# A GpSimd wait for VectorE's last latent split, ahead of the column sums of the later modulation vectors

## The chip, the cores and the metric

The kernel runs on one core of a Trainium2 chip. The metric is the device time of one execution in microseconds (us); lower is better. The core's engines each run their own instruction stream and meet at semaphores: TensorE (PE in the profile; PEld is its weight load), VectorE (DVE), ScalarE (ACT), GpSimd (POOL), and SyncE (SP), which only issues transfers here.

## The reference

Two layers of a diffusion backbone over 1024 latent tokens and 256 context tokens, model width 1024. Each layer has an adaLN modulation: six vectors (shift, scale, gate for the mixer and for the FFN) from one vector-matrix product.

```
m_lat = split(silu(c) @ w_mod[i] + b_mod[i], 6)          # i = 0, 1: 12 vectors of 1024
h_lat = rmsnorm(x_lat) * g_pre_mix * (1 + m_lat[1]) + m_lat[0]
y     = mla_mixer(h_lat, h_ctx, ...)   (layer 0)   |   conformer_conv(h_lat, ...)   (layer 1)
x_lat = x_lat + m_lat[2] * rmsnorm(y)
h     = modulate(rmsnorm(x_lat), m_lat[3], m_lat[4])
x_lat = x_lat + m_lat[5] * rmsnorm(conv_ffn(h, ...))
```

The latent attention of layer 0 projects `h` down (`w_dqkv`: 384 query latents, 128 key/value latents, 64 rotary), normalises these latents and projects them up for each of 8 heads; then softmax attention with 128-query blocks. Everything is fp32.

## The kernel before

Activations lie transposed, model blocks of 128 in the partitions, tokens in the free dimension. Matrix products are made of three fp32r matmuls (high*high, high*low, low*high): ScalarE rounds a tile to its high part, VectorE subtracts for the low part ("split"). `w_hi`/`w_lo`, `h_hi`/`h_lo` and `lat_hi`/`lat_lo` count these parts. `lat_lo` counts the low parts of the latents: two for the key/value side (L1461), then three for the query latents (L1470), five in all.

The twelve modulation vectors (shift, scale, ... of both layers) are computed in two ways. The first two, which the first norm needs, come at once: the scale on TensorE (L2028, counted by `mod_used`), the shift by VectorE's multiply-adds (L1402, L1405) and TensorE's column sums (L1983). The ten later ones, t = 0 to 9, are GpSimd's: for each of 8 row blocks of w_mod it loads 512 KB by a transfer of its own queue (L661 for the first two blocks, L679 for the others), multiplies it by a column of silu(c) in its partitions (L669, L671) and adds it to an accumulator (L672). When `mod_acc` reaches t + 1, TensorE sums the accumulator over the partitions (`mod_sums`, L1983, counted by `mod_mm`) and VectorE adds the bias. There are three accumulators' worth of order: t = 0 waits for `mod_mm` 1, t = 1 for 1, t = 2 for 2, t = 3 for 4, and so on.

TensorE asks for the first of them (`mod_acc` 1) in attention step 2, and for the next two (`mod_acc` 3) in step 4. There are 16 attention steps (8 heads, two halves of the queries); each has four blocks of scores (L2114, L2115 and the three lines of `three`), for which VectorE takes the row maxima (`maxes`, L1503), ScalarE the exponentials (L901), VectorE the scaling of the probabilities (`scales`, L1510 and L1511), TensorE the transposes (L2125), ScalarE and VectorE the split of the transposed (L778, L1517), TensorE the product with the values. Steps 0 and 1 have no product with values. The rotary fold (L2101) comes twice in each step with a new head's queries.

Ahead of attention VectorE makes `h`: for each of 8 blocks of the latents (`h_blocks`, 1024 tokens) the normalised block `ht` (L1379), of which ScalarE makes the high part (L813) and VectorE the low part (L1375); the order on VectorE is ht(k+1), low(k). TensorE's `first_two` follows these blocks: 6 matmuls of weight unit 0 for blocks 0 and 1, and 12 (units 0 and 1) for each later one, then the 12 that are left over. Then VectorE splits weight unit 2 (L1337) and does the same 8 blocks for the context (256 tokens). TensorE waits for all of these, multiplies the context (48 matmuls of 256 columns) and goes on with units 2 to 5, the statistics of the latents (L1957, L1976) and the first head's pieces.

GpSimd's stream begins so (L655 to L661); the diff touches it here:

```python
pool.wait_ge(silu_c, 2)
pool.wait_ge(mod_used, CB)
for t in range(10):
    for k in range(2):
        pool.dma_start(f(F_MD + k * L), modw[t + 2, k]).then_inc(mod_in[k], 16)
```

After the ten sums GpSimd adds squares for the norms and tile sums for the FFN; nothing of it starts before attention is over. The rest of the kernel (output projection, two FFNs, the convolution) is on TensorE's heels in the same manner.

Of the kernel before, what the change touches and what calls it, by code (L numbers as in the profile page):

```python
# [42 lines left out]
QLORA_B = 3  # L43
# [216 lines left out]
def build(nc, xT, ctxT, units, modw, vecs, ident_d, fold_d, cs_d, cosd_d, sind_d, outT):  # L260
# [7 lines left out]
    with ExitStack() as ctx:  # L268
# [13 lines left out]
        def sem(name):  # L282
            return ctx.enter_context(nc.semaphore(name))
# [18 lines left out]
        latent_in, mmx_done, rope_k, lat_scaled, lat_hi, lat_lo = (  # L302
            sem("latent_in"), sem("mmx_done"), sem("rope_k"), sem("lat_scaled"), sem("lat_hi"), sem("lat_lo"))
# [17 lines left out]
        def region(at, n):  # L321

            return next(start for _, start, end in REGIONS if start <= at and at + n <= end)
# [165 lines left out]
        def _(sp):  # L489
# [47 lines left out]
            def load_down(layer, turn, j, gated):  # L537

                d = dn_item(turn, j) + int(gated)
                if d < 8:  # L540
                    sp.wait_ge(w_lo, W_FFN[layer] + 6 + 7 * (MAIN - 2 + d // 4) + 6 + d // 2 % 2)
                else:
                    before = d - 8
                    at = 0 if before < 44 else 1 if before < 66 else 2 if before < 110 else 3
                    was = before - dn_item(at, 0)
                    if at % 2 or was % 2 == 0:
                        i = FB * at + (was if at % 2 else was // 2)
                        sp.wait_ge(w_lo, W_FFN[layer] + 139 + i + 1)
                    else:
                        sp.wait_ge(g_lo, 2 * FB * layer + FB * (at // 2) + was // 2 + 1)  # L550
                s, _, at = dn_landing(layer, d)
                if gated:
                    half = turn // 2
                    sp.wait_ge(g_out, 16 * (FB * layer + j + 1))
                    src = g_d[j][:, half * HALF:(half + 1) * HALF]
                else:
                    src = units[U_FFN[layer] + 2 * FB + j][:, turn % 2 * HALF:(turn % 2 + 1) * HALF]
                sp.dma_start(f(F_RAW + at, HALF), src).then_inc(dn_in[s], 16)
# [91 lines left out]
        def _(pool):  # L650
# [3 lines left out]

            pool.wait_ge(silu_c, 2)  # L655
            pool.wait_ge(mod_used, CB)


            for t in range(10):
# [1283 lines left out]
        def _(pe):  # L1943
# [359 lines left out]
            def ffn(layer, b):  # L2303
# [14 lines left out]
                for p in range(MAIN):  # L2318
                    m, bk = m0 + p, BANKS[p % 2]
                    for i, (_, _, which) in enumerate(PRODUCTS):  # L2320
                        pe.wait_ge(w_lo, w0 + 6 + 7 * p + i + 1)
                        if p == 0:
                            if i in (0, 1, 2):
                                pe.wait_ge(tap_g if i == 0 else tap_v, j0 + 2)
                            if i in (1, 2, 3, 6):
                                pe.wait_ge(b_lo, 16 * layer + {1: 8, 2: 4, 3: 12, 6: 16}[i])
                        elif p == 1 and i < 3:
                            pe.wait_ge(tap_g if i == 0 else tap_v, j0 + 3)
                        elif i == 0:
                            pe.wait_ge(s1_out, 5 * (m - 1))  # L2330
                        elif i == 1:
                            pe.wait_ge(c_new, 2 * (m - 1))
                        elif i == 2:
                            pe.wait_ge(c_new, 2 * (m - 1) - 1)
                        if i in (3, 4, 5, 6):
                            pe.wait_ge(s1_out, 5 * m + {3: 2, 4: 1, 5: 3, 6: 4}[i])
                        start = i < 3
                        for k in range(4):
                            mm = three(bank(bk[which]), half_unit(op_slot(p, i))[k], operands[i][k], start and k == 0, k == 3, True)
                        group_done(mm)  # L2340
# [192 lines left out]
```

## Time and profile before

| | |
|---|---|
| median of 3 runs | 2709.15 us (2703.23 to 2711.56) |
| the profiled execution's own time | 2706.82 us |
| its span in the trace | 2705.0 us |
| TensorE busy | 2574.6 us, 95% |
| VectorE busy | 1948.2 us, 72% |
| GpSimd busy | 902.1 us, 33% |
| share of the last chain on TensorE | 76% |

Busy times are sums over an engine's instructions. The chain is the work that ended last, followed back from the end: at each instruction to what released it or to the one before it on its engine. A TensorE row's duration overlaps the next row's, so its pace is read from the distance between starts.

### The profile page before, as it was taken

What the parts mean: (1) busy time and instruction counts of PE and PEld (TensorE: products, weight loads), DVE (VectorE), ACT (ScalarE), POOL (GpSimd) and SP (SyncE); (2) the same over time, 40 slices, a digit from 0 to 9 for tenths busy, and PEclk for the clock granted to TensorE, in tenths of its full rate; (3) what the DMA queues carried; (4) which work ended last, traced back from release to release, by engine and by line L of the source; (5) the groups of instructions that cost most, each with busy time, mean ns of one, the idle gap of its engine ahead of it and who ended that gap; (6) DMA issues with size and microseconds to landing.
All of it is one profiled execution on the core that took longest, in us unless ns stands there. A gap on an engine that the chain in (4) does not pass through costs nothing.

```text
span 2705.0 us, 31548 instructions
## 1 busy us (share of the span) xinstructions
PE 2574.6 (95%) x11674; PEld 2089.2 (77%) x11674; DVE 1948.2 (72%) x2071; ACT 1141.0 (42%) x1776; POOL 902.1 (33%) x590
## 2 busy tenths in 40 slices
PE   6789999999899999999999989997899999999997
PEld 5667888888687788888888866655787888888886
DVE  5826686867636999999436379997269999995352
ACT  2223444444533555555434232223435555554341
POOL 0801485862021566564001100000134675640001
PEclk9889999999999999999999999996999999999999
DMA  6400232331332222222645310001031222227362
GB/s 256 156 32 22 84 126 93 124 101 39 113 118 77 71 85 87 86 78 102 215 135 173 112 43 32 32 31 62 7 119 55 86 78 86 82 83 225 108 210 81
DMA packets 102356, 263.97 MB, mean 98 GB/s; under 512 B 11088, under 2 KB 12368, under 8 KB 102224
## 3 DMA queue, kind: packets, MB, share of 16 engines
q1 hardware_dynamic: 84496, 201.85, 22.1%
q0 software_dynamic: 11520, 41.95, 4.9%
q10 hardware_dynamic: 6208, 18.42, 1.8%
q8 instruction: 82, 1.34, 0.2%
q14 instruction: 50, 0.41, 0.0%
HBM read 218.13 MB, written 44.04 MB: 97 GB/s over the span
## 4 chain that ended last, share of the span: by engine, by line
PE 76%; DVE 17%; issue 4%; ACT 2%; DMA 1%; POOL 1%; POOLq 0%; ACTq 0%; DVEq 0%; SPq 0%
PE psum L1949 23%; PE psum L1951 22%; PE psum L1950 22%; DVE low L1874 7%; PE psum L2125 2%; PE psum L2200 1%; PE psum L2114 1%; PE psum L2115 1%; PE psum L1983 1%; DVE weights_f32r L1588 1%; DVE acts_f32r L1375 1%; PE psum L2398 1%; DMA low<-ctx_t 1%; DVE small L1503 1%; PE psum L2208 1%
## 5 line engine op out<-in xcount | busy, mean ns | idle before, releaser
L1949 PE MATMUL psum<-acts_f32r,weights_f32r 128*128 128x512 f32 x1760 | 702.5, 399 | 27.0 <-DVE acts_f32r L1375 10.2
L1951 PE MATMUL psum<-acts_f32r,weights_f32r 128*128 128x512 f32 x1760 | 693.1, 394 | 0.0
L1950 PE MATMUL psum<-acts_f32r,weights_f32r 128*128 128x512 f32 x1760 | 692.9, 394 | 0.0
L695 POOL TENSOR_TENSOR low<-low 128x512 f32<-128x512 f32 x70 | 101.5, 1451 | 1117.2 <-ACT low L992 1113.6
L778 ACT ACTIVATE weights_f32r<-low 128x512 fp32r<-128x512 f32 (+1 forms) x498 | 328.7, 669 | 339.9 <-PE psum L1951 261.0
L1949 PEld LDWEIGHTS psum<-acts_f32r,weights_f32r 128*128 128x128 f32 x1760 | 335.8, 191 | 105.0 <-DVE acts_f32r L1375 13.4
L1951 PEld LDWEIGHTS psum<-acts_f32r,weights_f32r 128*128 128x128 f32 x1760 | 334.8, 190 | 71.4
L1950 PEld LDWEIGHTS psum<-acts_f32r,weights_f32r 128*128 128x128 f32 x1760 | 335.5, 191 | 70.0 <-issue 1.9
L1721 DVE TENSOR_TENSOR weights_f32r<-low,weights_f32r 128x512 fp32r<-128x512 f32 x264 | 380.0, 1484 | 0.1
L1728 DVE TENSOR_TENSOR weights_f32r<-low,weights_f32r 128x512 fp32r<-128x512 f32 x176 | 124.5, 712 | 238.2 <-ACT weights_f32r L778 235.2
L722 POOL TENSOR_TENSOR low<-low 128x512 f32<-128x512 f32 x150 | 265.5, 1770 | 39.8 <-DVE acts_f32r L1706 29.3
L1874 DVE SCALAR_TENSOR_TENSOR low<-acts,vectors,low 128x1024 f32<-128x1024 f32 x169 | 203.4, 1277 | 11.6 <-ACT low L778 11.6
L778 ACT ACTIVATE low<-psum 128x512 f32<-128x512 f32 (+1 forms) x242 | 145.6, 601 | 145.3 <-PE psum L1951 144.9
L1949 PE MATMUL psum<-high_f32r,weights_f32r 128*128 128x512 f32 (+1 forms) x472 | 187.2, 397 | 15.7 <-DVE high_f32r L1375 6.9
L1950 PE MATMUL psum<-high_f32r,weights_f32r 128*128 128x512 f32 (+1 forms) x472 | 183.1, 388 | 0.0
L1951 PE MATMUL psum<-high_f32r,weights_f32r 128*128 128x512 f32 (+1 forms) x472 | 183.0, 388 | 0.0
L778 ACT ACTIVATE weights_f32r<-psum 128x512 fp32r<-128x512 f32 x160 | 92.7, 595 | 209.9 <-PE psum L2125 209.9
L1949 PE MATMUL psum<-acts_f32r,high_f32r 128*128 128x512 f32 x320 | 130.9, 409 | 15.7 <-ACT low L901 7.3
L745 POOL TENSOR_TENSOR low<-low 128x512 f32<-128x512 f32 x38 | 60.7, 1597 | 249.8 <-ACT low L778 249.8
L1503 DVE TENSOR_REDUCE small<-psum 128x1 f32<-128x1280 f32 x64 | 95.3, 1489 | 59.1 <-PE psum L2115 58.7
L1081 ACT ACTIVATE low<-low,vectors 128x1024 f32<-128x1024 f32 x76 | 94.6, 1247 | 76.6 <-DVE low L1792 56.1
L1517 DVE TENSOR_TENSOR weights_f32r<-psum,weights_f32r 128x512 fp32r<-128x512 f32 x160 | 107.6, 685 | 22.0 <-ACT weights_f32r L778 21.7
(196 smaller groups left out, 4717.3 us busy)
## 6 DMA issues: line engine op xcount, KB each, us to landing
low<-units SPq DMA_DIRECT2D x134, 512.0 KB, 4.1
low<-units SPq DMA_DIRECT2D x176, 256.0 KB, 3.7
set<-mod_w POOLq DMA_DIRECT2D x80, 512.0 KB, 3.9
gated<-low SPq DMA_DIRECT2D x44, 512.0 KB, 2.6
low<-gated SPq DMA_DIRECT2D x88, 256.0 KB, 4.2
residual<-low SPq DMA_DIRECT2D x48, 256.0 KB, 2.0
acts<-mod_w ACTq DMA_DIRECT2D x8, 1024.0 KB, 16.1
low<-x_t SPq DMA_DIRECT2D x4, 1024.0 KB, 27.8
```

The costliest lines, as they stand in the source:

```text
L695: pool.tensor_tensor(acc, first, ring(n), ADD).then_inc(sq_added, 1)
L722: pool.tensor_tensor(f(to[part - 1], HALF), x, y, op).then_inc(s_new, 1)
L778: return act.activation(out, in_, ACT.Copy, scale=scale)
L1081: act.activation(f(at), src, ACT.Identity, scale=V[:, wv + 2 * FB + c:wv + 2 * FB + c + 1], bias=V[:, wb + c:wb + c + 1]).then_inc(tap_mid, 1)
L1503: chain(dve.reduce_max(S[:, C_MX + c:C_MX + c + 1], PS[:, 0:KEYS], AX.X))
L1517: dve.tensor_tensor(r(at + HALF, HALF), bank(3 + kbn % 2), r(at, HALF), SUB).then_inc(tp_lo, 1)
L1721: dve.tensor_tensor(r(at + HALF, HALF), src, r(at, HALF), SUB).then_inc(w_lo, 1)
L1728: dve.tensor_tensor(r(at + HALF, HALF), dn_raw(layer, dn_item(turn, j)), r(at, HALF), SUB).then_inc(w_lo, 1)
L1874: chain.lag(dve.scalar_tensor_tensor(out=chained, in0=U[i % 2][:, t:t + L], scalar=V[:, V_WDW + t * CB + i:V_WDW + t * CB + i + 1], in1=ch ...
L1949: pe.matmul(out, wl, xh, start=first, stop=False, skip_group_check=continued)
L1950: pe.matmul(out, wh, xl, start=False, stop=False, skip_group_check=continued)
L1951: return pe.matmul(out, wh, xh, start=False, stop=last, skip_group_check=continued)
```

## The change

One line: before its first transfer, GpSimd also waits until VectorE has made the fifth and last low part of the latents (`lat_lo` = QLORA_B + 2 = 5).

```diff
             pool.wait_ge(silu_c, 2)
             pool.wait_ge(mod_used, CB)
+            pool.wait_ge(lat_lo, QLORA_B + 2)
 
 
             for t in range(10):
```

No instruction is added or removed besides the wait. All of GpSimd's work, its 80 transfers included, keeps its order behind it.

## Rows read from the trace of the kernel before

**Rows 1.** The page, busy time: us, share of the span, instructions.

```profile
PE 2574.6 (95%) x11674; PEld 2089.2 (77%) x11674; DVE 1948.2 (72%) x2071; ACT 1141.0 (42%) x1776; POOL 902.1 (33%) x590
```

**Rows 2.** The chain that ended last, 64 to 101 us: start, us, what.

```profile
67.92 1.28 DVE low L1379
69.20 3.23 DVE acts_f32r L1375
72.45 1.28 DVE low L1379
...
97.44 3.10 DVE weights_f32r L1337
```

**Rows 3.** Timeline of GpSimd: start, us, line, operation, tiles, idle before and its releaser.

```profile
68.96 2.37 POOL L672 TENSOR_TENSOR set<-set 128x1024 f32<-128x1024 f32 x1
...
99.76 1.13 POOL L661 DMA_DIRECT2D set<-mod_w  x2 [0.30 <-POOL set L672]
...
137.54 2.40 POOL L672 TENSOR_TENSOR high<-high,set 128x1024 f32<-128x1024 f32 x1
...
261.91 1.12 POOL L669 TENSOR_SCALAR set<-set,small 128x1024 f32<-128x1024 f32 x1 [120.55 <-PE psum L1983]
```

**Rows 4.** Timeline of VectorE, with the same columns.

```profile
49.86 2.47 DVE L1405 SCALAR_TENSOR_TENSOR high<-acts,small,high 128x1024 f32<-128x1024 f32 x2
...
102.03 0.48 DVE L1379 SCALAR_TENSOR_TENSOR low<-low,small,psum 128x256 f32<-128x256 f32 x1
...
102.94 0.48 DVE L1379 SCALAR_TENSOR_TENSOR low<-low,small,psum 128x256 f32<-128x256 f32 x1
...
108.05 2.45 DVE L1375 SCALAR_TENSOR_TENSOR high_f32r<-low,small,high_f32r 128x256 fp32r<-128x256 f32 x2
...
183.44 3.49 DVE L1470 TENSOR_TENSOR acts_f32r<-low,acts_f32r 128x1024 fp32r<-128x1024 f32 x3
```

**Rows 5.** Timeline of TensorE, with the same columns.

```profile
67.94 0.79 PE L1949 MATMUL psum<-acts_f32r,weights_f32r 128*128 128x512 f32 x1 [2.44 <-DVE acts_f32r L1375]
...
110.56 0.58 PE L1949 MATMUL psum<-high_f32r,weights_f32r 128*128 128x256 f32 x1 [6.89 <-DVE high_f32r L1375]
...
114.56 0.29 PE L1949 MATMUL psum<-high_f32r,weights_f32r 128*128 128x256 f32 x1
...
118.16 0.40 PE L1949 MATMUL psum<-acts_f32r,weights_f32r 128*128 128x512 f32 x1
...
129.07 2.29 PE L1957 MATMUL psum<-ones,low 128*128 128x1 f32 x20
```

**Rows 6.** Windows: busy us of PE, PEld, DVE, ACT, POOL; granted clock; DMA; GB/s.

```profile
70.00:80.00 10.00, 6.80 (x16) 4.42 (x15) 9.93 (x5) 2.68 (x3) 9.15 (x7) 0.50 0.35 117
```

**Rows 7.** VectorE's groups by form, 198 to 262 us: busy, mean ns; idle before.

```profile
L1503 DVE TENSOR_REDUCE small<-psum 128x1 f32<-128x1280 f32 x9 | 13.4, 1491 | 15.5 <-PE psum L2115 15.4
L1511 DVE TENSOR_SCALAR low<-low,small 128x1280 f32<-128x1280 f32 x8 | 7.1, 887 | 0.3
...
L1498 DVE TENSOR_TENSOR weights_f32r<-low,weights_f32r 128x1024 fp32r<-128x1024 f32 x1 | 1.2, 1225 | 0.2 <-ACT weights_f32r L778 0.2
```

**Rows 8.** VectorE's groups by form, 461 to 533 us.

```profile
L1511 DVE TENSOR_SCALAR low<-low,small 128x1280 f32<-128x1280 f32 x9 | 15.5, 1725 | 0.3
...
L1498 DVE TENSOR_TENSOR weights_f32r<-low,weights_f32r 128x1024 fp32r<-128x1024 f32 x1 | 3.0, 2983 | 0.0
```

**Rows 9.** The chain that ended last: rotary folds of four later attention steps.

```profile
476.54 0.86 PE psum L2101 x2
509.32 0.86 PE psum L2101 x2
...
609.11 0.86 PE psum L2101 x2
641.47 0.86 PE psum L2101 x2
```

**Rows 10.** The chain that ended last: TensorE's column sums of t = 1 and 2.

```profile
323.47 4.01 PE psum L1983 x32
```

## The prediction

> **What bounds the kernel now.** I read the page first, then the chain that ended last from 45 to 265 us, then the timelines of VectorE, GpSimd and TensorE over the same stretch. TensorE is busy 95% of the span [rows 1], so the time to gain is where TensorE stands still. The chain shows such a place: from 64 to 110 us it runs almost wholly on VectorE [rows 2]. TensorE gets the first block of `h` at 67.94, then works in bursts, and before the context matmuls at 110.56 it is idle for 6.89 us, released by VectorE's last low part [rows 5].
>
> In this stretch VectorE is slow. Between two `ht` (L1379) lie 72.45 - 67.92 = 4.53 us; `ht` itself takes 1.28, and the low part (L1375) 3.23 [rows 2]. The same operation on the same shape (scalar_tensor_tensor, two inputs in SBUF, 128x1024) took 2.47 us for two, about 1.24 each, at 50 us, when GpSimd had not begun [rows 4]. The difference fits GpSimd's rhythm. Its addition at 68.96 ends at 71.33 [rows 3]; the low part that starts at 69.20 ends at 72.43, that is 1.1 us after GpSimd's end: it waited out the addition and then ran. Seven such blocks have the same picture.
>
> After 110.56 the chain is on TensorE (context, units 2 to 5) until about 170 us, then a short tail over all engines, and VectorE's last low part of the latents ends at 183.44 + 3.49 = 186.9 [rows 4]. GpSimd meanwhile has finished t = 0 and t = 1 at 137.54 + 2.40 = 139.9 and stands for 120.55 us until TensorE has taken t = 0 in step 2 [rows 3]. So the two sums that slow VectorE down are made some 100 us before anybody wants them.
>
> **What the change does, part by part.**
>
> *It removes GpSimd from 48 to 187 us.* First VectorE's latent blocks. Undisturbed, `ht` and a low part take 2.47 [rows 4] plus some 0.03 of waiting on its own semaphore: 2.50 a pair. The third `ht` starts at 67.92 as before. Six pairs bring the low part of block 6 to 67.92 + 15.0 = 82.9; the last low part has to wait for ScalarE's high part (1.15 us a block in ScalarE's timeline, within the pair's 2.50) and ends at about 84.1. Then come the shift's bias and the split of unit 2, which ran from 97.44 for 3.10 us [rows 2] and took 1.23 undisturbed, by the like operation L1498 [rows 7]: it ends at about 85.6, against 100.54 before. The context blocks took from there to 108.05 + 2.45 = 110.50, 10.0 us [rows 4]. Their undisturbed pitch stands in the trace: 102.94 - 102.03 = 0.91 [rows 4]. First high part and `ht` 1.0, then seven low parts at 0.91 and the last, 7.5 in all: 93.1.
>
> TensorE has to keep up. `first_two` is 96 matmuls of 512 columns. At the full clock 48 of them took 129.07 - 118.16 = 10.91, 0.227 each [rows 5]. At the half clock 18 matmuls of 256 columns started in the 4.00 us from 110.56 to 114.56 [rows 5], 0.43 for 512. Now TensorE has the half clock all through 70 to 80 us (granted 0.50) [rows 6], since it stops after each block. With a block every 2.50 us, 6 matmuls at half clock take 2.6 and it does not stop. I take that the clock rises after 4 us of unbroken work, as it did from 110.56: then block 1 is done at 72.5, each later block costs 12 x 0.227 = 2.73, and the end is 72.9 + 6 x 2.73 + 2.73 = 92.0. That is 1.1 us before the context blocks, so VectorE still sets the moment, 93.2. Saved there: 110.56 - 93.2 = 17.4 us. Of the idle time only some 1.1 us is left, less than the pauses of 1.5 us at 84 to 95 us, through which the granted clock stayed at 0.98 to 1.00 in the windows. So the context matmuls should run at the full clock: 48 x 0.119 = 5.7 us instead of 118.16 - 110.56 = 7.6 [rows 5], 1.9 more. Sum: **19.3 us** earlier at unit 2. If the clock is low again it is 17.4.
>
> From 118 to 187 us nothing changes but the date. VectorE's operations that GpSimd disturbed there (120 to 137 us) are hidden behind TensorE, which had no gap. The things that could become late now: unit 3 and 4's transfers (issued when a slot is free, 4.3 us to land, needed 25 and more us later), the rotary tables (issued by ScalarE right after it copies the first result, 4.5 us to land, at about 99, needed at 110). None binds. GpSimd's own 16 transfers leave this stretch, which can only help.
>
> *It moves GpSimd's work to 168 us.* The last low part is now at 186.9 - 19.3 = 167.6. Behind the waiting instruction stand all transfers and sums; who waits for them is TensorE's column sums. One sum, t = 1, took from its first transfer at 99.76 to 139.94, 40.2 us with a disturbing VectorE [rows 3]. So t = 0 is ready at 208, t = 1 at 248, t = 2 at 288. They are wanted: t = 0 shortly before 261.91, when TensorE had summed it [rows 3], some 1.7 us of sums earlier, and 17 us less, at about 243; t = 1 and 2 at 323.47 [rows 10], less 17, at 306. Slack 35 and 18 us. t = 2 also waits for `mod_mm` 2, at 245, before 248. From t = 3 on GpSimd again waits for TensorE and all is as before. In time nothing is late.
>
> *The price: steps 0 and 1 of attention are now disturbed.* GpSimd was idle there, and now runs from 168 to 288 without a break. VectorE's operations with a PSUM input are no slower beside GpSimd (L1503, 1.49; L1517, 0.68 in either kind of stretch). Two operations are: `scales` (L1511), 0.887 undisturbed and 1.725 disturbed, and the split of a head's weights (L1498), 1.23 and 2.98 [rows 7, 8]. Steps 0 and 1 have eight and one: 8 x 0.84 + 1.75 = 8.5 us of VectorE's time. How much of it is on the path? In steps of full length hardly any: from fold to fold the step at 476.54, with GpSimd working, took 32.78, and the step at 609.11, with GpSimd idle for half of it, 32.36 [rows 9]. Steps 0 and 1 lack work on TensorE and are a chain of scores, maxima, exponentials; but VectorE waits for the scores 8 times, 15.4 us together, 5.7 of it the first time [rows 7], so about 1.4 per block is left as cover, with none in front of one of them (the one behind L1498). I take 1.5 us for that block, and 0.2 for each of the seven others, for the times when an operation waits longer than its cover: 3 us. The bounds are 0 and 8.5, and in the worst case each L1511 waits out a whole addition of 2.4.
>
> The skill has a rule on this that speaks against the change. The Trainium skill, "SBUF — State Buffer", section "Who interferes with whom", says that VectorE and GpSimd share one port pair with an exclusive lock: the later instruction blocks completely until the earlier one is done, and this holds for VectorE's two-input operations from SBUF and for its fast modes. The trace agrees: 3.23 us for the low part that met an addition, 1.24 without. By the lock at its worst all eight `scales` would meet one; the measured mean says that they meet about a third of it.
>
> *Sum.* 19.3 - 3.0 = 16.3 us. The profiled execution's own time was 2706.82: 2690.5. The median of the three runs is 2.3 above that execution, in a spread of 8.3; I say **2691**.
>
> **The rivals.**
>
> A. *Only part of the gain* (0.12). TensorE takes over as the bound in `first_two`: its clock does not rise at once, or falls again. Were it at half clock all through, 96 x 0.43 = 41 us from 67.94 would end at 109, and nearly nothing is left of the gain; with a rise at 80 as now, 28 matmuls are done by then and 68 more take 15.4, end 95.5, 2.4 late, and the context runs cold: about 15 - 3 = 12, 2695 to 2697. For it: the half clock of [rows 6]. Against: that clock goes with the pauses which the change takes away, and it rose 4.0 us after 110.56 [rows 5].
>
> B. *The disturbance is moved, not removed* (slower or even; 0.07). In steps 0 and 1 an L1511 that starts just behind an addition waits for all of it, 2.4 us; VectorE is in order, so the next maximum is late, so the exponential, so the scores. 8 x 2.4 + 1.75 = 21 us, less nothing if TensorE has no other work, makes 2706.8 - 19.3 + 21 = 2708.5. It decides the sign from 2.2 us a block on. Against: a mean of 0.84 in 9 disturbed cases [rows 8] and about 1.4 of cover.
>
> C. *The sums come too late* (slower; 0.03). If a sum takes over 46 us instead of 40.2, TensorE waits at 306 for t = 2; with 52 us a sum it waits 18 us, the whole gain, and beyond that the kernel is slower. For it: GpSimd now meets VectorE in every step. Against: t = 2 to 9 were made in attention, and take 37 us in GpSimd's timeline.
>
> D. *No effect* (0.03): VectorE is slow here for another reason than GpSimd. Then about 2707. Against: the durations beside GpSimd's, one by one.
>
> **How the numbers follow.** My forecast has 0.75: 2686 to 2696, from the price of 0 to 8.5 and the clock's 1.9, and the spread of runs. Rival A 0.12 (2695 to 2702), B 0.07 (2700 to 2712), C 0.03, D 0.03. The range that holds 8 in 10 is 2684 to 2700. A measurement of this kernel tells 0.3%, 8.1 us, from no change. Faster by that: the forecast and most of A, 0.84. Within: part of A and B, D, 0.11. Slower: the worse part of B and C, 0.05.
>
> **What the profile after would show.** L1375 at 1.3 us a block from 67 us on, and L1337 at 1.2; the context matmuls starting at 93 us and unit 2 at 99; TensorE's granted clock over 0.9 from 72 us on; GpSimd's first L669 at about 171 us; L1511 in steps 0 and 1 at a mean of 1.7; the column sums at 243 and 307 with no wait for GpSimd. I am wrong if TensorE's last matmul of `first_two` comes after 94 us (A), if steps 0 and 1 take more than 8 us longer (B), or if a column sum waits (C).

## The result and the profile after

The changed kernel took 2688.84 us in the median of 7 runs (2684.0 to 2694.01), the kernel before 2709.15 (2703.23 to 2711.79, 7 runs). The ratio is 0.9924, interval [0.9908, 0.9941]: 0.8% faster, 20.3 us by the medians. Forecast were 2691 and a range of 2684 to 2700. The profiled execution has a span of 2687.0 us against 2705.0: 18.0 us less.

The line of the page that answers to [rows 1]; VectorE's busy time is 13.9 us lower with the same instructions:

```profile
PE 2567.0 (96%) x11674; PEld 2085.8 (78%) x11674; DVE 1934.3 (72%) x2071; ACT 1140.9 (42%) x1776; POOL 897.9 (33%) x590
```

All line numbers are one higher from here on. VectorE's timeline in the `h` blocks, the answer to [rows 2] and [rows 4]:

```profile
68.01 1.28 DVE L1380 SCALAR_TENSOR_TENSOR low<-low,small,psum 128x1024 f32<-128x1024 f32 x1
69.21 1.28 DVE L1376 SCALAR_TENSOR_TENSOR acts_f32r<-low,small,acts_f32r 128x1024 fp32r<-128x1024 f32 x1
70.53 1.28 DVE L1380 SCALAR_TENSOR_TENSOR low<-low,small,psum 128x1024 f32<-128x1024 f32 x1
...
81.78 2.59 DVE L1376 SCALAR_TENSOR_TENSOR acts_f32r<-low,small,acts_f32r 128x1024 fp32r<-128x1024 f32 x2
...
84.60 1.23 DVE L1338 TENSOR_TENSOR weights_f32r<-low,weights_f32r 128x1024 fp32r<-128x1024 f32 x1
```

The low part takes 1.28 us instead of 3.23, the pair 70.53 - 68.01 = 2.52, the split of unit 2 1.23 instead of 3.10. TensorE's timeline, the answer to [rows 5], and below it the windows that answer to [rows 6]:

```profile
68.03 0.80 PE L1950 MATMUL psum<-acts_f32r,weights_f32r 128*128 128x512 f32 x1 [2.10 <-DVE acts_f32r L1376]
...
92.00 0.39 PE L1952 MATMUL psum<-acts_f32r,weights_f32r 128*128 128x512 f32 x1
93.48 0.39 PE L1950 MATMUL psum<-high_f32r,weights_f32r 128*128 128x256 f32 x1 [1.09 <-DVE high_f32r L1376]
...
99.33 0.40 PE L1950 MATMUL psum<-acts_f32r,weights_f32r 128*128 128x512 f32 x1
...
110.24 2.29 PE L1958 MATMUL psum<-ones,low 128*128 128x1 f32 x20
```

```profile
70.00:80.00 10.00, 9.44 (x40) 7.29 (x39) 9.86 (x9) 4.56 (x5) 0.00 (x0) 0.94 0.01 2
80.00:90.00 10.00, 10.00 (x46) 8.29 (x45) 9.58 (x15) 4.91 (x8) 0.00 (x0) 1.00 0.18 52
90.00:100.00 10.00, 8.91 (x62) 8.08 (x61) 6.02 (x12) 5.36 (x9) 0.00 (x0) 1.00 0.47 160
```

TensorE's wait ahead of the context has shrunk from 6.89 to 1.09 us, and the granted clock from 70 to 80 us is 0.94 instead of 0.50. GpSimd's timeline, the answer to [rows 3]:

```profile
166.66 1.29 POOL L662 DMA_DIRECT2D set<-mod_w  x2 [166.20 <-DVE acts_f32r L1471]
...
204.00 1.13 POOL L662 DMA_DIRECT2D set<-mod_w  x2 [0.30 <-POOL set L673]
...
241.46 1.74 POOL L662 DMA_DIRECT2D set<-mod_w  x2 [0.30 <-POOL high L673]
...
279.11 1.13 POOL L662 DMA_DIRECT2D set<-mod_w  x2 [0.30 <-POOL set L673]
...
305.61 1.12 POOL L670 TENSOR_SCALAR set<-set,small 128x1024 f32<-128x1024 f32 x1 [25.38 <-PE psum L1984]
```

It starts when VectorE's last low part is done and works until 279, with pauses of at most 2.9 us for its own transfers. Then it waits for TensorE, not TensorE for it. VectorE's groups by form from 176 to 242 us, the stretch that was undisturbed in [rows 7]:

```profile
L1504 DVE TENSOR_REDUCE small<-psum 128x1 f32<-128x1280 f32 x9 | 13.4, 1488 | 11.0 <-PE psum L2116 11.0
L1512 DVE TENSOR_SCALAR low<-low,small 128x1280 f32<-128x1280 f32 x8 | 12.3, 1542 | 0.3
...
L1499 DVE TENSOR_TENSOR weights_f32r<-low,weights_f32r 128x1024 fp32r<-128x1024 f32 x1 | 2.4, 2432 | 0.2 <-ACT weights_f32r L779 0.2
```

The scaling of the probabilities has gone from 0.887 to 1.54 us and the split of the head's weights from 1.23 to 2.43: the disturbance is here now.

**Where the 18.0 us lie.** The instructions and their order are the same in both traces, so each VectorE and ScalarE instruction can be set against itself. The table gives by how many us it starts earlier than in the first trace of before, as the median over the stretch (times of the kernel before; of an even number of instructions, the upper of the two in the middle). Three traces are of the changed kernel itself, one is a second of the kernel before; the others are told of below.

| stretch, us | before, 2nd | changed | changed, 2nd | changed, 3rd | wait_h | t1_late |
|---|---|---|---|---|---|---|
| 98 to 103 | 0.1 | 14.7 | 14.7 | 14.6 | 14.6 | 14.6 |
| 110 to 120 | -0.1 | 18.8 | 18.9 | 18.7 | 18.7 | 18.7 |
| 150 to 165 | -0.1 | 20.4 | 20.4 | 20.3 | 20.3 | 18.7 |
| 200 to 215 (step 0) | 0.1 | 22.0 | 20.3 | 20.1 | 19.1 | 20.2 |
| 240 to 270 (step 2) | 0.1 | 22.4 | 15.8 | 15.7 | 19.1 | 20.3 |
| 600 to 700 | 3.2 | 22.9 | 21.6 | 19.7 | 18.7 | 26.7 |
| 1870 to 1895 | -0.1 | 23.1 | 20.0 | 19.8 | 15.1 | 25.1 |
| 1930 to 2000 | 0.1 | 19.7 | 20.0 | 16.4 | 15.6 | 23.9 |
| 2600 to 2650 | 0.0 | 19.7 | 20.0 | 16.4 | 12.1 | 20.4 |

The gain is complete before attention and is the same in all three traces of the changed kernel, 20.3 to 20.4 us. One run more bears on it: `late_start` of experiment 3 does the same work as the changed kernel up to 166 us, and it is 19.0 us ahead at 110 to 120 us but 18.9 at 150 to 165. What comes after attention begins moves by several us from one execution to the next, in the kernel before too.

### The profile page after: what moved, and what is told of

It reads as the page before. It is cut to its first block, busy times and chain, and to the rows that moved or that the text cites. A ratio compares the mean times of both kernels' runs of the same rounds, so it can differ in the third digit from the quotient of the medians.

```text
span 2687.0 us, 31548 instructions
## 1 busy us (share of the span) xinstructions
PE 2567.0 (96%) x11674; PEld 2085.8 (78%) x11674; DVE 1934.3 (72%) x2071; ACT 1140.9 (42%) x1776; POOL 897.9 (33%) x590
## 4 chain that ended last, share of the span: by engine, by line
PE 76%; DVE 16%; issue 4%; ACT 2%; DMA 1%; POOL 1%; ACTq 0%; POOLq 0%; DVEq 0%; SPq 0%
PE psum L1950 23%; PE psum L1952 22%; PE psum L1951 22%; DVE low L1875 7%; PE psum L2126 2%; PE psum L2201 1%; PE psum L2115 1%; PE psum L2116 1%; DVE weights_f32r L1589 1%; PE psum L1984 1%; PE psum L2399 1%; DVE small L1504 1%; DMA low<-ctx_t 1%; PE psum L2209 1%; DVE high_f32r L1710 1%
## 5 line engine op out<-in xcount | busy, mean ns | idle before, releaser
L1950 PE MATMUL psum<-acts_f32r,weights_f32r 128*128 128x512 f32 x1760 | 703.2, 400 | 19.3 <-DVE acts_f32r L1648 6.4
L673 POOL TENSOR_TENSOR set<-set 128x1024 f32<-128x1024 f32 x49 | 120.2, 2453 | 4.1
```

Of the source, the lines that this page charges most:

```text
L673: add = pool.tensor_tensor(acc, acc, part, ADD)
L1950: pe.matmul(out, wl, xh, start=first, stop=False, skip_group_check=continued)
```

## The experiments

**1. Which part of GpSimd's work slows VectorE.** Three kernels put a piece of work ahead of the new wait, from 65 us on, and leave the sums after it. Their results are not used. The waits on `mod_in` further down count the transfers that each adds.

Transfers alone:

```diff
+            pool.wait_ge(mod_mm, 1)
+            for k in range(16):
+                if k > 1:
+                    pool.wait_ge(mod_in[k % 2], 16 * (k // 2))
+                pool.dma_start(f(F_MD + (k % 2) * L), modw[2, k % CB]).then_inc(mod_in[k % 2], 16)
+            for k in range(2):
+                pool.wait_ge(mod_in[k], 16 * 8)
             pool.wait_ge(lat_lo, QLORA_B + 2)
```

> The changed kernel, with 16 extra transfers of 512 KB on GpSimd's queue from 65 us on, ahead of the new wait, and no arithmetic; the sums are made later, as in the changed kernel. Theory 1 (GpSimd's arithmetic holds up VectorE's two-input operations): the low parts of h stay at 1.28 us each, the context matmuls start at 93 to 94 us, the time is that of the changed kernel within 2 us (2685 to 2692). Rival (the transfers or the making of their descriptors slow VectorE): the low parts come to 2 us or more and the context matmuls start after 98.

Additions alone, and one-input multiplications alone. Each diff is cut to the work that is added; ahead of it stand two transfers that fill its inputs, the waits for them, and the wait for `mod_mm` 1:

```diff
+            for k in range(12):
+                chain(pool.tensor_tensor(f(F_MD + 2 * L), f(F_MD), f(F_MD + L), ADD))
             pool.wait_ge(lat_lo, QLORA_B + 2)
```

```diff
+            for k in range(24):
+                chain(pool.tensor_scalar(f(F_MD + 2 * L), f(F_MD), S[:, C_SC:C_SC + 1], 1.0, MUL, MUL))
             pool.wait_ge(lat_lo, QLORA_B + 2)
```

> The changed kernel, with 12 extra additions (128x1024, two inputs in SBUF, results not used) on GpSimd from 65 us on, ahead of the new wait, and two transfers before them. Theory 1: each low part beside them waits for the addition that runs, so it takes 2.5 to 3.5 us instead of 1.28; 12 additions of 2.4 us cover 65 to 95 us, and the context matmuls start at 103 to 110 us. Most of the gain of the change is gone: 2695 to 2705. Rival (it was the transfers): the low parts stay at 1.3 and the context starts at 93 to 94.

> The changed kernel, with 24 extra one-input multiplications by a column (128x1024, results not used) on GpSimd from 65 us on, ahead of the new wait, and two transfers before them. Theory 1 in the form that any GpSimd instruction which reads SBUF holds up a two-input operation of VectorE: each low part waits for the rest of one of 1.1 us, 0.6 on average, and takes about 1.9 us; eight of them put the context at 97 to 100 us, 4 to 6 us later than in the changed kernel. Rival: only GpSimd's two-input additions hold VectorE up; then the low parts stay at 1.3 and the context starts at 93 to 94.

The latent low parts (L1383 here) among VectorE's groups by form, 64 to 115 us, and the first context matmul in TensorE's timeline. Transfers:

```profile
L1383 DVE SCALAR_TENSOR_TENSOR acts_f32r<-low,small,acts_f32r 128x1024 fp32r<-128x1024 f32 x8 | 10.2, 1281 | 0.1
```

```profile
93.51 0.38 PE L1957 MATMUL psum<-high_f32r,weights_f32r 128*128 128x256 f32 x1 [1.00 <-DVE high_f32r L1383]
```

Additions, with GpSimd's own row last:

```profile
L1383 DVE SCALAR_TENSOR_TENSOR acts_f32r<-low,small,acts_f32r 128x1024 fp32r<-128x1024 f32 x8 | 17.3, 2167 | 0.0
```

```profile
108.38 0.58 PE L1957 MATMUL psum<-high_f32r,weights_f32r 128*128 128x256 f32 x1 [10.99 <-DVE high_f32r L1383]
```

```profile
67.70 36.93 POOL L663 TENSOR_TENSOR set<-set 128x1024 f32<-128x1024 f32 x12 [17.98 <-PE psum L1991]
```

Multiplications:

```profile
L1383 DVE SCALAR_TENSOR_TENSOR acts_f32r<-low,small,acts_f32r 128x1024 fp32r<-128x1024 f32 x8 | 15.8, 1984 | 0.0
```

```profile
102.36 0.58 PE L1957 MATMUL psum<-high_f32r,weights_f32r 128*128 128x256 f32 x1 [5.95 <-DVE high_f32r L1383]
```

```profile
66.06 37.24 POOL L663 TENSOR_SCALAR set<-set,small 128x1024 f32<-128x1024 f32 x24 [16.31 <-PE psum L1991]
```

Sixteen transfers leave the low part at 1.281 us and the start where the changed kernel has it. The additions put the start back to 108.4, within 2.2 us of the kernel before, and the multiplications to 102.4. So it is the arithmetic, and both kinds of it; the rivals fall. VectorE's `ht`, the same operation on the same shape but with one input in PSUM, stays at 1.28 beside the additions:

```profile
L1387 DVE SCALAR_TENSOR_TENSOR low<-low,small,psum 128x1024 f32<-128x1024 f32 x8 | 10.2, 1280 | 3.7 <-PE psum L1984 3.5
```

My sizes were off in part: the mean beside additions is 2.17, below the 2.5 to 3.5 expected, but the blocking goes both ways, so 12 additions spread over 36.9 us (a mean of 3.01 us for one, not 2.4) and disturbed VectorE longer, into the context blocks. The same holds for the multiplications, 1.46 on average, not 1.12, and their start at 102.4 is later than the 97 to 100 expected.

The times of the three were 2698.19, 2712.74 and 2695.32 us, one execution each. The first and the second are 6 and 8 us above what was expected, and the third is faster than the first although its context starts 9 us later. Part of this is what happened later: in step 1 of attention alone the first two lost 1.8 and 4.1 us and the third gained 0.7 against the kernel before (experiment 4). In the measure of the table the first is 20.4 us ahead at 150 to 165 us, like the changed kernel, and 9.9 at the end; what its other losses come from stays open. The times are therefore no evidence for the theory; the durations and the starts are.

**2. The context blocks by themselves.** GpSimd begins when the latent `h` is done:

```diff
-            pool.wait_ge(lat_lo, QLORA_B + 2)
+            pool.wait_ge(h_lo, CB)
```

> The new wait is put earlier still: GpSimd waits for the low parts of the latent h alone (h_lo 8, at 84 us), so its first products and additions, from about 88 us on, stand beside the eight context blocks only. Port theory: the latent part of the gain stays (VectorE's latent blocks end at 84.4), of the context part (8 blocks, 10.0 us disturbed, 7.5 undisturbed) some 1.5 to 2.5 us are lost, and the context matmuls start at 94.5 to 96 instead of 93.5. Rival (it is the first minutes of GpSimd's work in general, transfers included, that cost): the start falls back to 100 or later.

TensorE's timeline:

```profile
95.95 0.39 PE L1950 MATMUL psum<-high_f32r,weights_f32r 128*128 128x256 f32 x1 [3.50 <-DVE high_f32r L1376]
```

2.5 us later than in the changed kernel, as large as the context's term in the sum (10.0 - 7.5). The time was 2696.42 us, one execution. In the measure of the table it is 14.8 us ahead at 150 to 165 us, 5.6 less than the changed kernel, and not 2.5 less: after the pause of 3.50 us the granted clock was at half speed from 97.1 to 100.5, in the context, and after the column sums again from 117.6 to 121.0. In this execution the longer wait ahead of the context cost more than itself.

**3. How much slack the sums have.** GpSimd begins about 42 us later than in the changed kernel, when it has the fourth exponential of step 0:

```diff
-            pool.wait_ge(lat_lo, QLORA_B + 2)
+            pool.wait_ge(s_free, 4)
```

> The new wait is put later: GpSimd waits for the fourth exponential of attention step 0 (s_free 4, at about 205 us), some 38 us later than in the changed kernel. Rival C of my prediction made real: sum t = 0 would be ready at about 243, wanted at 237.5, so TensorE waits 5 us for it; the sums t = 1 and 2 at about 318 against 303, another 10 to 15 us. Expected 15 to 20 us slower than the changed kernel's 2687 span, 2700 to 2708. If the slack was larger than I read from the rows, TensorE waits less and the time stays under 2695.

The time was 2708.84 us, one execution, the span 2707.0. TensorE's waits from 190 to 400 us (us in total, times, longest), its column sums after the two waits, and GpSimd's transfers for the first three sums:

```profile
PE psum L1984 <- POOL set L673: 13.0, 2, 8.4
```

```profile
245.90 2.30 PE L1984 MATMUL psum<-ones,set 128*128 128x1 f32 x11 [4.58 <-POOL set L673]
...
321.12 3.58 PE L1984 MATMUL psum<-ones,high 128*128 128x1 f32 x16 [8.39 <-POOL set L673]
```

```profile
208.29 1.28 POOL L662 DMA_DIRECT2D set<-mod_w  x2 [207.84 <-ACT low L902]
...
246.14 1.13 POOL L662 DMA_DIRECT2D set<-mod_w  x2 [0.30 <-POOL set L673]
...
284.56 1.13 POOL L662 DMA_DIRECT2D set<-mod_w  x2 [0.30 <-POOL high L673]
```

Rival C is real once the wait is late enough: TensorE waits 4.6 us for t = 0, which was ready at 245.8 and wanted at 241.3 (the column sums of the changed kernel start at 237.5, but step 2 begins 3.7 us later here), and 8.4 us for t = 2, ready at 321.1. In the measure of the table it is 18.7 us ahead of before at 240 to 270 us, 10.7 at 270 to 300, and 0.2 at 340 to 400: the second step is more than the wait, since the clock was at half speed after each wait, from 246.2 to 253.0 and from 317.8 to 331.5 us (the step with the two sums took 46.6 us, against 36.3 in before). In the changed kernel t = 0 was ready at 204 and t = 2 at 279, and TensorE's sums, which stood at 323.47 in [rows 10], began at 301.8; so the slack was 34 and 23 us, near the 35 and 18 of the prediction.

**4. Other places for the two sums, and the price in attention.** Three variants keep the `h` blocks free, and move what meets attention:

```diff
-            pool.wait_ge(lat_lo, QLORA_B + 2)
+            pool.wait_ge(h_lo, 2 * CB)
```

is wait_h; split_sums and t1_late have this and one more wait ahead of the transfers of t = 1:

```diff
             for t in range(10):
+                if t == 1:
+                    pool.wait_ge(lat_lo, QLORA_B + 2)      # split_sums
+                    pool.wait_ge(s_free, 6)                # t1_late, in place of it
                 for k in range(2):
```

> The new wait is put earlier: GpSimd waits for the low parts of h and of the context's h (h_lo 16) instead of the last low part of the latents, so it works from 93 to about 168 us and is idle in attention steps 0 and 1, as before the change. Theory 1 with the price of my prediction: the context matmuls start at 93 to 94 as in the changed kernel; steps 0 and 1 get back what the disturbance cost there (3 us by the prediction, under 1 by the trace after); but t = 1 now meets the tail before attention (152 to 166 us), where VectorE's two-input splits of the latents are on the path, 1 to 4 us. Sum 2684 to 2692, even with the changed kernel within 3 us, and clearly faster than before (ratio about 0.993). Rival (the place of the work in attention is what matters, not the h blocks): it falls back to about 2705.

> t = 0 starts after the low parts of h and of the context's h (h_lo 16, 93 us) and runs beside TensorE-bound work until 131 us; t = 1 waits for the last low part of the latents and runs from 166 to 204 us, beside step 0 only. Port theory: the context starts at 93 to 94 as in the changed kernel, the tail before attention is undisturbed, step 1 of attention is undisturbed. Even with the changed kernel or 1 to 2 us better: 2684 to 2690. The clock's half-speed stretches in attention and later can move it by 5 us either way, as they do between runs of one kernel.

> t = 0 starts after the low parts of h and of the context's h (93 us) and ends at 131; t = 1 waits for the sixth exponential of attention (s_free 6, in the middle of step 1, about 217 us) and ends at about 255, t = 2 at about 292, wanted at 303. So the h blocks, the tail before attention, step 0 and half of step 1 are all undisturbed, and no sum is late. Theory: step 1 takes the 30.1 us that it takes undisturbed, the milestones are 20.4 us ahead of before at 165 us and stay within 1 us of that in steps 1 to 4. Against the changed kernel no difference beyond the spread of runs: 2684 to 2692. Rival (the disturbance of steps 0 and 1 costs several us on average): 2 to 3 us below the changed kernel in the medians of one chip.

The changed kernel and the kernel before were run again:

> The changed kernel itself, once more, with a second trace. Theory 2 (the differences of some us after attention's start, such as the 3.3 us that the changed kernel loses at 1880 us, are where the granted clock happens to fall, not the change): the two traces agree within 0.3 us up to the first stretch at the half clock that only one of them has, and differ by about half of each such stretch from there on, 1.7 or 3.4 us at a time; the spans differ by up to 10 us. Rival (the loss at 1880 us comes from the change): it stands in this trace at the same place.

> The changed kernel itself, timed beside the others on the same chip: median 2684 to 2692, ratio to before 0.991 to 0.994, and a third trace. Up to 165 us it is 20.4 us ahead of before, as in both earlier traces, within 0.3 us. Attention step 1 takes 29.5 to 34.6 us, according to how long its clock is low.

> The kernel before, with a second trace, to see how far its own milestones move. The same theory as for the changed kernel: the disturbed low parts at 2.9 us on average, context matmuls at 110.4 to 110.7; step 1, undisturbed, 30.1 us; differences of 1.7 or 3.4 us where a stretch at the half clock is longer or missing; span 2698 to 2712.

| kernel | median, us (lowest to highest, runs) | ratio to before on its chip |
|---|---|---|
| wait_h | 2693.50 (2685.20 to 2695.49, 6) | 0.9929 [0.9913, 0.9946] |
| split_sums | 2691.78 (2686.84 to 2696.42, 6) | 0.9938 [0.9921, 0.9954] |
| t1_late | 2689.81 (2682.33 to 2692.86, 6) | 0.9934 [0.9915, 0.9952] |
| changed, timed again beside t1_late | 2692.54 (2691.59 to 2698.33, 6) | 0.9951 [0.9933, 0.9968] |
| changed, 2nd trace | 2686.83, one execution | |
| before, 2nd trace | 2706.84, one execution | |

All keep the gain, so the place of the work in attention is not what the change is about. None is shown to be better than the others: the intervals overlap. The changed kernel beside t1_late came out slightly above what was expected (2684 to 2692, ratio 0.991 to 0.994).

What the disturbance costs in attention is read from step 1, from its rotary fold to that of step 2 (L2101 of the kernel before). The windows, with [rows 6]'s columns, of before, then of the changed kernel's first and second trace, then of t1_late, where GpSimd comes in only at the end:

```profile
212.78:242.88 30.10, 26.56 (x139) 22.10 (x140) 18.64 (x29) 11.55 (x20) 0.00 (x0) 0.94 0.06 18
```

```profile
190.80:220.48 29.68, 24.98 (x139) 20.98 (x140) 21.93 (x28) 11.56 (x20) 24.50 (x19) 1.00 0.39 127
```

```profile
192.51:227.10 34.59, 28.90 (x139) 23.92 (x140) 23.02 (x28) 11.56 (x20) 29.01 (x22) 0.85 0.40 126
```

```profile
192.60:222.60 30.00, 26.46 (x140) 22.07 (x141) 18.67 (x29) 11.54 (x20) 1.21 (x2) 0.94 0.06 18
```

Undisturbed, step 1 takes 30.0 to 30.1 us in both traces of before, in wait_h, wait_h8 and t1_late, at a granted clock of 0.94. Disturbed, it takes 29.7 us where the clock stays at full speed and 34.6 where it falls to a mean of 0.85; the third trace of the changed kernel has 34.5, add_early 34.2, xfers_early 31.9, scale_early 29.4. The mean of the changed kernel's three is 32.9, so the price is 2.8 us, and anything from -0.4 to +4.5 in one execution.

Two runs lie in between. In late_start GpSimd's arithmetic begins at 212.3, in the second half of the step, which takes 30.1 us. In split_sums it ends at 204.8 and rests until 245.9; step 1 was expected to be undisturbed there, but its first 12 us are not, and it takes 34.3 us:

```profile
192.59:226.91 34.32, 29.14 (x140) 24.20 (x140) 20.94 (x29) 11.54 (x20) 12.67 (x9) 0.85 0.23 76
```

So GpSimd's work in the rest of the step adds next to nothing (34.3 against 34.6 and 34.5), and the length of the step goes with its granted clock. Whether the disturbance of the first 12 us makes the clock fall, or it would have fallen without it, these runs do not show; the price of 2.8 us is a mean of three executions, and not shown to be due to VectorE's longer operations.

The other places cost too: in wait_h t = 1 meets the tail before attention, and 20.3 us ahead have become 19.1 by step 0. t1_late, which avoids both, keeps its lead through the first steps (later it moves, to 26.7 us and back to 20.4, and not within the 1 us that was expected for steps 1 to 4); it is 2.7 us below the changed kernel by the medians of one chip, in the direction of the price, but not clear of noise.

**5. The loss at 1900 us.** In the first trace of the changed kernel 3.3 us of the lead go between 1895 and 1940 us (of before). There TensorE sums over partitions with 24 one-column matmuls (L2399). Its timeline in the first trace and in the second:

```profile
1878.06 3.14 PE L2399 MATMUL psum<-ones,low 128*128 128x1 f32 x24
1881.06 0.78 PE L1950 MATMUL psum<-acts_f32r,weights_f32r 128*128 128x512 f32 x1
1881.63 0.63 PE L1951 MATMUL psum<-acts_f32r,weights_f32r 128*128 128x512 f32 x1
1882.06 0.63 PE L1952 MATMUL psum<-acts_f32r,weights_f32r 128*128 128x512 f32 x1
```

```profile
1881.04 2.73 PE L2399 MATMUL psum<-ones,low 128*128 128x1 f32 x24
1883.64 0.49 PE L1950 MATMUL psum<-acts_f32r,weights_f32r 128*128 128x512 f32 x1
1883.96 0.40 PE L1951 MATMUL psum<-acts_f32r,weights_f32r 128*128 128x512 f32 x1
1884.20 0.40 PE L1952 MATMUL psum<-acts_f32r,weights_f32r 128*128 128x512 f32 x1
```

After the same instructions the clock is at half speed in one execution (0.43 us from one matmul to the next) and at full speed in the other (0.23). The second trace loses nothing there; the third does. So the loss is no fixed cost of the change: theory 2 stands, the rival of after_again falls. That the change does not make it likelier is not shown: two of its three traces have the loss, and neither of the two of before.

## Why the prediction was right, point by point

**The place and the mechanism** were right. VectorE set the start of the context, and its low parts waited for GpSimd's arithmetic. The rows after and experiment 1 show it: GpSimd's transfers alone do not have the effect, its additions and multiplications do.

**The terms ahead of attention** fit closely. Low part of the last latent block done at 84.4 (84.1 in the sum), split of unit 2 at 85.8 (85.6), last matmul of `first_two` starting at 92.0 (its end put at 92.0), context at 93.5 (93.2), unit 2 at 99.3. 118.16 - 99.33 = 18.8 us against 19.3. Rival A did not come: the clock rose when the pauses were gone, at 71.1 us in the first trace, 3.1 us after the first matmul. The 4 us of the prediction are no constant: in the second trace of the changed kernel the clock rose at 74.0, 6.0 us after the first matmul, and the last of `first_two` started at 92.5. The context still started at 93.45, since VectorE set that moment.

**One thing was missing from this sum.** From 118 to 187 us I had nothing but a shift. The changed kernel is 20.4 us ahead at 150 us, 1.6 more than at 118. After the column sums of the key statistics (L1957 at 129.07 [rows 5]) the clock was at half speed in both traces of before (131.6 to 135.1 us in the first), and in none of the three of the changed kernel. wait_h and t1_late are one and the same up to there, and from 112 to 116 us the granted clock is 1.00 in wait_h and 0.74 in t1_late, which is the one with 18.7 us. late_start, which is the changed kernel up to 166 us, has the half clock from 113.0 to 116.4 and 18.9 us. So the 1.6 us can come and go as the loss of experiment 5 does, and without them the change is worth 18.7 to 19.0 us ahead of attention, within 0.6 of the 19.3 of the sum. Whether the change makes the full clock likelier there stays open.

**The price in attention**, 3 us between 0 and 8.5, was the uncertain term. In the profiled execution it was nothing: the lead grew from 20.4 to 21.9 us by the fold of step 0 and to 22.4 by step 2. Over three traces of the changed kernel step 1 has a mean price of 2.8 us. That this is near 3 is luck: I had put the 3 together from VectorE's cover in front of the maxima, while the single executions have -0.4, 4.5 and 4.4, according to TensorE's clock in the step. Rival B, in which the price grows to the whole gain, did not come; 4.5 us was the most seen in the changed kernel. Rival D, that GpSimd is not what slows VectorE, falls with the durations.

**The deadlines** held, with 34 and 23 us to spare, and experiment 3 shows what rival C would have cost. (The transfers that the prediction calls those of units 3 and 4 are those of 4 and 5; they bound nothing.) **After attention** the prediction let the lead pass to the end unchanged. The three traces end 18.0, 20.0 and 14.7 us ahead (spans of 2687.0, 2685.0 and 2690.3 against 2705.0 twice), mean 17.6, against the 16.3 of the sum. The 18.0 of the profiled execution is 20.4 before attention, 2.7 that it gained from there to 1895 us (2.0 of it by step 2), and 5.1 that went later, 3.3 of them at 1900 us and 1.7 at the very end, where its granted clock is 0.93 from 2660 to 2670 us and before's, over the same work (2678 to 2688), 1.00. So it came near the 16.3 of the sum by errors that cancel: 1.1 us more ahead of attention, 5.7 more from there to 1895 us (2.7 gained where 3.0 were to be lost), 5.1 less after that. How large the spread is that the clock alone makes is not settled; six and seven runs of the changed kernel on two chips have medians of 2692.5 and 2688.8.

## What to carry to other kernels

When one engine's background work has slack, look at what its instructions do to the others' while they run, not only at when the result is wanted: two sums made 100 us too early cost 20 us, at the one place where VectorE set the pace. Look for an operation whose duration differs between stretches of one trace, set its undisturbed duration in the sum, and check that the next engine can keep that pace. To judge a change of under 1%, line up the same instructions of two traces and take a second trace of each kernel: a loss that one execution has and the next has not is no fixed cost of either.

## What the runs showed of the hardware that was not expected

The blocking is mutual, and a one-input multiplication of GpSimd does it nearly as much as an addition: beside back-to-back multiplications the low part took 1.98 us, beside additions 2.17, alone 1.28; GpSimd's own went from 1.12 to 1.46 and from 2.4 to 3.01 on average. In the kernel before the low parts had 2.93 on average (its groups by form), more than beside back-to-back additions. There the two engines had fallen into step, with a period of 4.5 us: from 69.12 to 91.82 six low parts began 0.15 to 0.16 us behind an addition of GpSimd, and so waited out nearly all of it.

After a run of one-column matmuls (20 to 24 of them, 2.3 to 3.1 us) TensorE may be at half clock or not, in the same program at the same place, and the work behind it is 1.6 to 3.3 us later when it is.
